# Two blocks of VectorE code and one of ScalarE's change places in a hybrid decoder kernel: RWKV's shifts and the mLSTM's gates

## The reference, cut to what matters

```python
def _token_shift(p, mu):
    prev = jnp.pad(p, ((0, 0), (1, 0), (0, 0)))[:, :-1]
    return p + (prev - p) * mu

p = _token_shift(p, mu)
r, k, v, wd, ad = split(p)
decay = exp(-exp(-softplus(-(w0 + tanh(wd) @ w_up)) - 0.5))
a = sigmoid(a0 + ad @ a_up)
v = v + (v_first - v) * sigmoid(v0 + (v @ v_dn) @ v_up)      # from the second layer on
```

```python
i_pre = ig + i_b
log_f = log_sigmoid(fg + f_b)
b = cumsum(log_f)              # the kernel keeps one running sum over all tokens
m = running_max(i_pre - b)     # and one running maximum
```

## Time and profile before

| | |
|---|---|
| median of three runs | 2257.98 us |
| the profiled execution's own time | 2258.79 us |
| its span, first to last instruction | 2257.0 us |
| TensorE matmuls busy | 2222.0 us (98%) |
| GpSimd busy | 1743.7 us (77%) |
| VectorE busy | 1104.7 us (49%) |
| ScalarE busy | 664.7 us (29%) |
| granted TensorE clock | 0.998 |

### The profile page before, as it was taken

One profiled execution on the slowest core, in us unless ns is written; L12 is line 12 of the kernel. 1 busy time (PEld: TensorE's weight loads), 2 busy tenths in 40 slices (PEclk: granted clock), 3 DMA queues, 4 the chain that ended last, 5 costly groups with the idle time before them and its releaser, 6 DMA issues. The chain is left out here.

```text
span 2257.0 us, 35480 instructions
## 1 busy us (share of the span) xinstructions
PE 2222.0 (98%) x14528; PEld 1710.1 (76%) x14528; DVE 1104.7 (49%) x1481; ACT 664.7 (29%) x1211; POOL 1743.7 (77%) x1228
## 2 busy tenths in 40 slices
PE   7999999999999999999999999999999999999998
PEld 6767777777777778777777677767777777777777
DVE  6123227666564762555250223376676647625542
ACT  4222322222322332442341232223133223324421
POOL 3677679678688989888547776896797799898884
PEclk9999999999999999999999999999999999999999
DMA  4722344333334546622445232433343255466223
GB/s 164 194 84 84 98 146 119 103 101 106 89 108 161 156 140 202 233 91 82 145 122 164 83 105 84 149 109 100 95 119 98 86 180 157 126 217 219 95 78 125
DMA packets 165475, 288.44 MB, mean 128 GB/s; under 512 B 28792, under 2 KB 36344, under 8 KB 163776
## 3 DMA queue, kind: packets, MB, share of 16 engines
q1 hardware_dynamic: 125216, 211.60, 31.3%
q10 hardware_dynamic: 40096, 74.57, 9.9%
HBM read 234.43 MB, written 51.68 MB: 127 GB/s over the span
## 5 line engine op out<-in xcount | busy, mean ns | idle before, releaser
L754 POOL TENSOR_SCALAR w_hi<-raw 128x512 fp32r<-128x512 f32 x552 | 905.4, 1640 | 316.0 <-PE ps_proj L795 270.0
L764 POOL TENSOR_TENSOR w_lo<-raw,w_hi 128x512 fp32r<-128x512 f32 (+1 forms) x640 | 843.9, 1319 | 150.0 <-ACT w_hi L1231 94.6
L795 PE MATMUL ps_proj<-h_hi,w_hi 128*128 128x512 f32 (+1 forms) x1760 | 724.7, 412 | 5.9 <-POOL w_lo L764 2.9
L795 PE MATMUL ps_proj<-h_lo,w_hi 128*128 128x512 f32 (+1 forms) x1760 | 688.8, 391 | 0.2 <-DVE h_lo L1773 0.2
L795 PE MATMUL ps_proj<-h_hi,w_lo 128*128 128x512 f32 x1728 | 675.7, 391 | 0.0
L795 PEld LDWEIGHTS ps_proj<-h_hi,w_hi 128*128 128x128 f32 (+1 forms) x1760 | 329.7, 187 | 104.6 <-issue 27.1
L795 PEld LDWEIGHTS ps_proj<-h_lo,w_hi 128*128 128x128 f32 (+1 forms) x1760 | 329.5, 187 | 73.9 <-DVE h_lo L1773 0.6
L795 PEld LDWEIGHTS ps_proj<-h_hi,w_lo 128*128 128x128 f32 x1728 | 325.8, 189 | 66.3 <-issue 7.7
L810 PE MATMUL ps_proj<-w_hi,h_hi 128*128 128x512 f32 x448 | 181.3, 405 | 0.4 <-POOL w_lo L764 0.4
L810 PE MATMUL ps_proj<-w_lo,h_hi 128*128 128x512 f32 x448 | 174.8, 390 | 0.0
L810 PE MATMUL ps_proj<-w_hi,h_lo 128*128 128x512 f32 x448 | 174.8, 390 | 0.0
(11 more groups left out here) (348 smaller groups left out, 2884.5 us busy)
## 6 DMA issues: line engine op xcount, KB each, us to landing
raw<-in_w_in_dram SPq DMA_DIRECT2D x480, 256.0 KB, 2.7
raw<-in_w_out_dram SPq DMA_DIRECT2D x128, 256.0 KB, 3.0
projected<-stage SPq DMA_DIRECT2D x116, 256.0 KB, 2.8
arena<-projected ACTq DMA_DIRECT2D x90, 256.0 KB, 3.0
out_dram<-arena ACTq DMA_DIRECT2D x7, 1024.0 KB, 4.8
gated_hi<-arena ACTq DMA_DIRECT2D x24, 256.0 KB, 2.6
gated_lo<-arena ACTq DMA_DIRECT2D x24, 256.0 KB, 3.1
h_hi<-gated_hi SPq DMA_DIRECT2D x8, 768.0 KB, 5.8
```

Of the source, the lines that this page charges most:

```text
L754: nc.gpsimd.tensor_scalar(hi, src, 1.0, None, ALU.mult).then_inc(s_hi_split, 1)
L764: nc.gpsimd.tensor_tensor(lo, src, hi.bitcast(F32), ALU.subtract).then_inc(s_raw_split, 1)
L795: last = mm(ps_proj[rows, m, :], lhsT, rhs, start=(k == 0 and j == 0), stop=(k == KT - 1 and j == len(products) - 1))
```

## The change

On VectorE the shifts of `rw_lora` and `rw_v` move ahead of the gate part. On ScalarE the gates' exponential and logarithm move from ahead of the keys' copies to behind the issue of the loads of receptance and key. No operation is added or taken away in the source.

```diff
@@ ScalarE
                     act.dma_start(rw_v[:, 2:4, 1:T + 1], ...).then_inc(s_rw_first_loaded, 16)
-                    act.wait_ge(s_ml_gate_abs, 1)
-                    link(nc.scalar.activation(ml_sg[32:36, :], ml_sg[32:36, :], ACT.Exp, scale=-1.0))
-                    nc.scalar.activation(ml_sg[32:36, :], ml_sg[32:36, :], ACT.Ln, bias=1.0).then_inc(s_ml_gate_log, 1)
                     fill("to_k")
                     act.wait_ge(s_rw_shifted, 1)
                     nc.scalar.activation(rw_lora[0:32, 1:T + 1], rw_lora[0:32, 1:T + 1], ACT.Tanh).then_inc(s_rw_lora_tanh, 1)
                     wait_stored(G_K)
                     act.dma_start(rw_in[:, 0, 1:T + 1], p_dram[4 * G_R]).then_inc(s_rw_rk_loaded, 16)
                     act.dma_start(rw_in[:, 1, 1:T + 1], p_dram[4 * G_K]).then_inc(s_rw_rk_loaded, 16)
+                    act.wait_ge(s_ml_gate_abs, 1)
+                    link(nc.scalar.activation(ml_sg[32:36, :], ml_sg[32:36, :], ACT.Exp, scale=-1.0))
+                    nc.scalar.activation(ml_sg[32:36, :], ml_sg[32:36, :], ACT.Ln, bias=1.0).then_inc(s_ml_gate_log, 1)
                     act.wait_ge(s_ml_gates, 1)
@@ VectorE
                     gates, forget = slice(0, 36), slice(32, 36)
+                    dve.wait_ge(s_rw_first_loaded, 16 * rw_loads)
+                    shift(rw_lora, col("rw_mu", 12), slice(0, 64)).then_inc(s_rw_shifted, 1)
+                    dve.wait_ge(s_rw_shifted, 1)
+                    for j in range(4):
+                        ins = shift(rw_v[:, j, :], col("rw_mu", 8 + j))
+                        if j < 3:
+                            link(ins)
+                    ins.then_inc(s_rw_v_shifted, 1)
                     dve.wait_ge(s_ml_gate_cleared, 1)
...
                     v.scalar_tensor_tensor(out=ml_rows[heads, 1, :], in0=ml_sg[heads, :], scalar=-1.0, in1=ml_rows[heads, 0, :], op0=MUL, op1=SUB).then_inc(s_ml_gates, 1)
-                    dve.wait_ge(s_rw_first_loaded, 16 * rw_loads)
-                    shift(rw_lora, col("rw_mu", 12), slice(0, 64)).then_inc(s_rw_shifted, 1)
-                    dve.wait_ge(s_rw_shifted, 1)
-                    for j in range(4):
-                        ins = shift(rw_v[:, j, :], col("rw_mu", 8 + j))
-                        if j < 3:
-                            link(ins)
-                    ins.then_inc(s_rw_v_shifted, 1)
```

## The result

| | before | changed |
|---|---|---|
| median | 2257.96 us (8 runs) | 2263.95 us (8 runs) |
| profiled execution | 2258.79 us | 2263.76 us |
| its span | 2257.0 us | 2262.0 us |
| granted clock, mean | 0.998 | 0.995 |
| ratio | | 1.003 [1.002, 1.0039] |

The changed kernel is slower by 0.3% [0.2%, 0.39%]. The forecast was +2.9 us, +6.0 us was measured; the direction was right and the time is inside the range, but the size is twice what was forecast, and slower by over 0.2% had got only 0.22. The mean granted clock fell, which no step of the forecast had. One of the eight executions took 2274.07 us at a mean clock of 0.945; without it the median is 2263.76 us.

What follows compares the result with a forecast made beforehand. TensorE, busy 98% of the span, was taken as the bound, so only its idle time counts. Layer 0's wait +5.2, refund -2.2 and layer 1's -0.1 gave +2.9 us, 2260.9 us on the median; range for 8 of 10, 2256.9 to 2264.2 us.

Steps and rivals of the forecast that it cites:

- slower by over 0.2%: Whole kernel: a slowdown of at least +4.5 us, chance 0.22; within 0.2% had 0.75, faster by over 0.2% had 0.03.
- The wait, 5.2 us: Layer 0, line 987: TensorE waits for line 1870 until 372.4 instead of starting at 367.17, +5.2 us.
- The refund, -2.2 us: Layer 0, lines 987 to 991: GpSimd gets ahead during TensorE's wait, so its lateness there goes, -2.2 us.
- if the distance from 987 to 991 stays at 21 us: Layer 0: a sign that the forecast is wrong; it expected these lines 19 us apart.
- no refund: Layer 0, behind 987: GpSimd stays late and the 26 tiles take 21.0 us again; +5.1, 2263.1 us; chance 0.17.
- -0.1 forecast: Layer 1: the 2.40 us wait at line 972 goes but comes back before 980; -0.1 us taken.
- No wait at 972, about 3 us before 980: Layer 1, TensorE: the 2.40 us wait goes; the one before 980 grows from 0.78, released by VectorE's copy.
- the forecast's own sign of error: Layer 1: the forecast is wrong if line 980 moves by more than 1 us.
- The forecast's 7.8 us: Layer 1: time from issue to landing of the last load of values, the later of 6.7 to 7.8 us.
- slow table switch: Both layers' new ScalarE chains: each switch costs 1.4 us more than the row shows; +5.5, 2263.5 us; chance 0.04.
- Less contention: Both layers: VectorE's operations fall better against GpSimd's, 2.2 us less per layer; -2.4, 2255.6 us at its end; chance 0.12.
- Hidden: Layer 0: exponential starts well before 355.5 or margin at 987 is larger; both layers keep their time, 2258.0 us; chance 0.07.

Runs made afterwards that it cites:

- e2: The new order in layer 0 alone, the old order in layer 1, against the kernel before: 2261.82 us, ratio 1.0013 [1.0004, 1.0022].
- e11: The new order in layer 0 alone, run again against the kernel before: 2261.22 us, ratio 1.0013 [1.0004, 1.0021].
- e5: The changed kernel run again, against the kernel before: 2262.60 us, ratio 1.0020 [1.0010, 1.0029].
- e10: The changed kernel run a third time, against the kernel before: 2263.56 us, ratio 1.0021 [1.0012, 1.0030].
- e1: The new order in layer 1 alone, the old order in layer 0, against the kernel before: 2258.91 us, ratio 1.0002 [0.9993, 1.0011].
- e4: The kernel before with seven idle-work VectorE operations added ahead of line 1867 in layer 0: 2263.84 us, ratio 1.0023 [1.0013, 1.0032].
- e7: The kernel before with six gate operations moved off VectorE's chain, ScalarE's 1449, 1450 and their store into the second pass: 2255.28 us, ratio 0.9976.
- e8: The kernel before with four idle-work VectorE operations added ahead of line 1867 in layer 0: 2261.00 us, ratio 1.0007 [0.9998, 1.0016].
- e3: The kernel before with only VectorE's shifts moved, ScalarE's exponential left ahead of the keys' copies: 2269.98 us, ratio 1.0052 [1.0038, 1.0066].
- e6: The changed kernel with six TensorE tiles of layer 0 moved from behind line 987 to between 980 and 987: 2258.82 us, ratio 0.9998 against before.
- e9: The changed kernel with six layer 0 tiles moved ahead of 987 and five layer 1 tiles moved between 972 and 980: 2259.95 us, ratio 1.0001 against before.

## Why the prediction was wrong

What the forecast put at nothing is TensorE's clock: it priced a wait of 5 us and let the engine go on behind it as if it had not stood. That alone doesn't make +6.0 us of +2.9: in layer 0 another error cancels it, and some 2 us more, treated last, are not located.

**Layer 0: +3.0 forecast (5.2 - 2.2), 3.2 us in the profile and 2.9 us timed alone (e2, e11).** The sum was right by luck, through two errors that cancel: line 987 started 2.3 us too early for the forecast, and 991 followed it 2.5 us too late.
- *The wait, 5.2 us.* Measured from line 980, TensorE was to go on at 987 after 16.7 us (372.4 - 355.7) and did after 14.4 (371.55 - 357.11), so 2.3 us sooner. One half is line 1852, 1.3 us behind line 980 (358.42 - 357.11) instead of 2.4, and 0.9 to 1.0 in e2, e5, e10 and e11. The gate is the load of receptance, as forecast, but the stores ahead of it landed in 2.0 to 2.1 us in these profiles, so it went out 2.6 us ahead of line 980 (357.11 - 354.55) where it had been 1.1. The earlier trace rows was the slowest of the old order's profiles; e1, e4, e7 and e8 have 2.1 to 3.0 us. The other half is 1867 to 1870, which took 5.56 us instead of 6.70, within the forecast's bounds, whose lower end was some 4.4 us. The wait itself shrank only to 4.25 us, because TensorE was ready 1.3 us sooner too: 10.2 us behind line 980 (367.30 - 357.11), where it had been 11.5 (367.17 - 355.70) with two waits for GpSimd in them. So part of GpSimd's refund fell ahead of 987.
- *The refund, -2.2 us.* This is the step that failed. Its mechanism was right: no wait for GpSimd stands between 987 and 991, and at a granted clock of 1.00 they are 18.6 us apart (e3). But behind waits of 3.8 to 7.2 us the granted clock fell to the 1.2 GHz level, for 3.4 to 5.6 us of the work that follows, and 987 to 991 took 20.3 to 21.4 us in seven profiles (the changed kernel, e2, e4, e5, e8, e10, e11). That costs 1.7 to 2.8 us, most of the refund or more than it. In the profile of the changed kernel the parts close: 32.5 us from 980 to 991 before, +4.25 for the wait, -1.3 and -2.5 for GpSimd's waits ahead of and behind 987, +2.7 for the clock, 35.7 us. The forecast named its own test, "if the distance from 987 to 991 stays at 21 us", and it did.

The rival *no refund* (chance 0.17) had the right distance by the wrong cause: it said that GpSimd would stay late, and that isn't so.

**Layer 1: -0.1 forecast.** "No wait at 972, about 3 us before 980" holds: 2.9 (changed kernel), 3.5 (e1, e5), 5.5 (e10). Timed alone the layer costs 1.0002 [0.9993, 1.0011], which is nothing, as forecast. Counted from the start of the keys' copies, line 980 moved by less than 1 us in the changed kernel, e1 and e5, and by 2.0 us in e10, which is past the forecast's own sign of error. And the argument left out two things.
- VectorE has no slack left. Before, its chain had 3.78 us of idling before the copy; in the new order it starts with the values' loads and runs without idling but for the logarithm. So what delays its start delays line 980, and the second of these loads took 6.6 us (changed kernel), 7.6 and 7.8 (e1, e5) and 9.1 us (e10) from issue to landing. The forecast's 7.8 us is the middle one of the 13 profiles.
- The clock falls here too. In all six profiles with the new order in this layer (changed, e1, e5, e6, e9, e10) TensorE waits 2.9 to 5.5 us before line 980, and in all six the granted clock falls behind it; in the changed kernel, e5 and e10 it is 0.69, 0.66 and 0.67 from 1490 to 1495 us. Behind the old order's 2.40 us before 972, in the kernel before and e4, it stayed at 1.00, but behind 3.63 us there, in e11, it fell as well.

From the start of the keys' copies to line 991 the old order took 42.6 to 45.8 us in five profiles, 44.2 in the kernel before; the new order took 44.2 (changed), 44.7 (e1), 44.8 (e5), 47.2 (e6), 47.3 (e9) and 47.8 us (e10). The means are 44.0 and 46.0 us, and each order's spread is larger than that difference. The changed kernel's 44.2 us is the lowest of the new order, so that its first profile shows this layer as free is in part luck.

**The whole is not fully explained.** The three measurements of the changed kernel lie near +5.3 us together, the two layers timed alone give 2.9 + 0.5 = 3.4 us. The 2 us between are as large as the intervals, so whether the layers add or work on each other stays open.

The granted clocks of all executions say what kind of time it is. Their mean is 0.9981 over the 89 executions of the kernel before that ran beside the experiments, 0.9978 with the new order in layer 1 alone, 0.9967 in layer 0 alone (e2 and e11), and 0.9954 in the changed kernel (e5 and e10). Times the span the loss against the kernel before gives an estimate of 0.6, 3.2 and 6.1 us lost to the clock, a bit too much since the clock during a wait counts too. So the 2 us that the parts lack are there in the clock as well. At a mean clock of 0.996 both kernels take about the same, 2262.0 us (3 executions) and 2262.6 (8). This goes together and doesn't yet say in which stretch the clock was lost. One place was looked at: behind a wait of 2.21 us near 1087 us, at the layers' boundary, the clock sometimes falls, which costs about 1.5 us. It fell in the changed kernel, e3, e5, e6, e7, e8, e9 and e11, and not in before, e1, e2, e4 and e10. The fastest kernel has the drop and e10 has not, so it isn't tied to the change; whether it comes more often with it, one profile of each can't say. The 1.4 us at the start were in the profiles of e5 and e7 and not in that of e10 (line 980 at 357.22, 357.17 and 356.04), so they aren't tied to it either.

The rival *slow table switch* is out: VectorE's idling around exponential, load and logarithm is 2.64 us, as in the earlier trace rows. The Trainium skill ("ScalarE: Activation LUTs", section "What ACT_TABLE_LOAD costs") puts a drain of some 1.4 us beside each switch, and the changed kernel's trace doesn't show it in the new place either. *Less contention* is half seen, 1.1 us at 1867 to 1870, and doesn't decide. *Hidden* is out: the wait at 987 is there in every profile with the new order in layer 0 and no filler.

## What to carry to other kernels

A wait taken from TensorE came back here at its next operation that needs the same late engine; it went when work left that engine's chain. Reordering VectorE cost 3 to 6 us, and taking six operations out of the chain won 4. A wait on TensorE is priced with the clock behind it: here 1.7 to 2.8 us more for one of 3.8 us or longer, so a sum of waits alone is too low, and a refund that falls right behind a wait is not to be counted in full. Tiles that are to fill a wait must come from behind it.

## What the runs showed of the hardware

- TensorE's granted clock went to its 1.2 GHz level during or behind all 16 single waits of 2.9 to 8.9 us in these two stages, over 11 profiles; matmuls then follow each other every 0.43 us instead of 0.23, for 3.4 to 5.8 us. Behind 2.21 us at the boundary it fell in 8 of 13 profiles. Behind 1.06 us before line 987 in e1 it did not.
- In the profile of the changed kernel the time lost to the clock isn't in the list of waits: TensorE counts as 6.00 us busy in 6.00 us (15 matmuls). Only the count and the granted clock show it.
- The same load of values in layer 1 took between 6.6 (changed kernel) and 9.1 us (e10) to land, over 13 profiles. The keys' four stores in layer 0 took 3.2 to 3.5 us in the kernel before and 2.0 in the changed one.
- The table load in front of line 1449 ran from 358.40 to 359.68 us while its activation waited until 366.03: a switch ahead of a waiting instruction cost nothing.
